# A complex scan over 63 chunk states rebuilt as a tree, with its transposes and spills moved, in a one-core decoder layer

## What is computed

```python
def combine(e1, e2):
    a1r, a1i, b1r, b1i = e1
    a2r, a2i, b2r, b2i = e2
    return (a2r * a1r - a2i * a1i, a2r * a1i + a2i * a1r,
            a2r * b1r - a2i * b1i + b2r, a2r * b1i + a2i * b1r + b2i)
_, _, hr, hi = lax.associative_scan(combine, (ar_full, ai_full, bu_re, bu_im), axis=1)
y = einsum('btgp,gcp->btgc', hr, c_re) - einsum('btgp,gcp->btgc', hi, c_im)
...
y_act = gelu(y_ssm)
```

## Time and profile before

| what | value |
|---|---|
| median of three runs | 922.96 us (922.57 to 925.85) |
| the profiled execution | 927.62 us, its span 925.9 us |
| PE busy (matmul) | 906.0 us, 98% of the span |
| PE busy (weight loads) | 882.5 us, 95% |
| DVE busy | 603.8 us, 65% |
| ACT busy | 443.2 us, 48% |
| POOL busy | 97.0 us, 10% |
| mean granted clock of TensorE | 0.996 |

### The profile page before, as it was taken

The page is one execution under the profiler, slowest core; times in us unless marked ns, Lnnn a source line. Parts: engine busy times, 40 slices in busy tenths (PEclk is TensorE's granted clock), DMA queues, the critical chain, the costliest instruction groups (busy, mean ns, idle before and its releaser), DMA issues.

```text
span 925.9 us, 17543 instructions
## 1 busy us (share of the span) xinstructions
PE 906.0 (98%) x7350; PEld 882.5 (95%) x7350; DVE 603.8 (65%) x815; ACT 443.2 (48%) x663; POOL 97.0 (10%) x151
## 2 busy tenths in 40 slices
PE   6999999998999999999999999999999999999998
PEld 5999998998999889999999999999999999999998
DVE  6689699810777746474568666666676666778453
ACT  7446333233876544544356544444444444446532
POOL 5390036102001210100000000000000000000000
PEclk9999999999999999999999999999999999999999
DMA  8521579844423576522323322223323223242202
GB/s 229 131 83 45 155 214 189 198 117 131 124 72 100 194 274 217 171 69 71 90 69 92 92 88 83 86 88 91 92 76 94 84 91 91 92 137 71 70 4 99
DMA packets 135333, 105.71 MB, mean 114 GB/s; under 512 B 18688, under 2 KB 124536, under 8 KB 134968
## 3 DMA queue, kind: packets, MB, share of 16 engines
q1 hardware_dynamic: 129096, 83.38, 30.6%
q0 software_dynamic: 6064, 21.19, 8.0%
q10 hardware_dynamic: 96, 0.04, 0.0%
HBM read 90.48 MB, written 13.98 MB: 113 GB/s over the span
## 4 chain that ended last, share of the span: by engine, by line
PE 88%; DVE 6%; ACT 3%; issue 1%; DMA 1%; SPq 0%; ACTq 0%; DVEq 0%; POOLq 0%
PE dense L2324 62%; PE banks L2324 19%; PE scoreA L2324 3%; PE banks L2511 2%; DVE Hb L1750 1%; DVE sc L1750 1%; DMA xtok<-in_x_prompt 1%; PE scoreB L2324 1%; ACT whi L1361 1%; DVE wlo L1774 1%; DVE Llo L1774 1%; ACT t L1655 1%; DVE t L2148 1%; DMA y_spill<-ygelu 0%; DVE Ssum L1750 0%
## 5 line engine op out<-in xcount | busy, mean ns | idle before, releaser
L1774 DVE TENSOR_TENSOR wlo<-wraw,whi 128x1024 fp32r<-128x1024 f32 (+2 forms) x139 | 152.7, 1103 | 108.9 <-ACT whi L1361 96.9
L2324 PE MATMUL dense<-hid,whi 128*128 128x256 f32 (+1 forms) x1024 | 176.5, 294 | 0.1
L2324 PE MATMUL dense<-act_hi,whi 128*128 128x256 f32 (+1 forms) x736 | 168.5, 300 | 2.5 <-DVE wlo L1774 2.2
L2324 PE MATMUL dense<-act_hi,wlo 128*128 128x256 f32 (+1 forms) x736 | 164.5, 295 | 0.0
L2324 PE MATMUL dense<-act_lo,whi 128*128 128x256 f32 (+1 forms) x736 | 164.3, 295 | 0.0
L2324 PEld LDWEIGHTS dense<-hid,whi 128*128 128x128 f32 x1024 | 152.3, 187 | 0.5 <-issue 0.5
L1361 ACT CAST whi<-wraw 128x1024 fp32r<-128x1024 f32 x100 | 109.9, 1101 | 45.6 <-PE banks L2324 44.1
L2324 PEld LDWEIGHTS dense<-act_hi,whi 128*128 128x128 f32 x736 | 125.0, 190 | 5.7 <-DVE wlo L1774 2.4
L2324 PEld LDWEIGHTS dense<-act_lo,whi 128*128 128x128 f32 x736 | 125.3, 189 | 0.0
L2324 PEld LDWEIGHTS dense<-act_hi,wlo 128*128 128x128 f32 x736 | 125.1, 189 | 0.0
L2324 PE MATMUL dense<-hid,wlo 128*128 128x256 f32 (+1 forms) x512 | 108.8, 293 | 0.0
(11 more groups left out here) (375 smaller groups left out, 1592.9 us busy)
## 6 DMA issues: line engine op xcount, KB each, us to landing
wraw<-in_w_in SPq DMA_DIRECT2D x32, 512.0 KB, 5.7
wraw<-in_w_up SPq DMA_DIRECT2D x32, 512.0 KB, 4.1
wraw<-in_w_down SPq DMA_DIRECT2D x32, 512.0 KB, 4.2
gates_spill<-gst POOLq DMA_DIRECT2D x16, 288.0 KB, 3.3
page<-in_cache_k SPq DMA_DIRECT2D x16, 256.0 KB, 8.7
page<-in_cache_v SPq DMA_DIRECT2D x16, 256.0 KB, 7.3
wraw<-in_w_out SPq DMA_DIRECT2D x8, 512.0 KB, 4.1
wraw<-in_w_ple_gate SPq DMA_DIRECT2D x8, 512.0 KB, 4.1
```

Of the source, the lines that this page charges most:

```text
L1774: return nc.vector.tensor_tensor(out=lo, in0=whole, in1=f32(hi), op=ALU.subtract)
L2324: return nc.tensor.matmul(out, lhsT, rhs, start=start, stop=stop, skip_group_check=True)
```

## The change

The scan becomes a tree: five levels up (distance 1 to 16) and five down (16 to 1), each over every 2d-th position only. Up, the destinations are 2d, 4d, ...; down, 3d, 5d, .... The counts n are 31, 15, 7, 3, 1 and 1, 3, 7, 15, 31, together 114. The ten steps are spread over the same five first places of the schedule as (0), (1, 2), (3, 4, 5, 6), (7, 8), (9), and the sixth place has none; `final` moves up by one place. The states go out after unit 18, and come in after unit 20; two whole units that stood between them and the first `y` now stand behind `sfinal`, ahead of the `vout` transposes. After the last `y` the first half of a unit is begun. POOL makes one power less, and the counts awaited on `scanned` follow.

```diff
+SCANS = 10
...
-        event("scan", lvl)
-        if lvl == 5:
+        for step in ((0,), (1, 2), (3, 4, 5, 6), (7, 8), (9,), ())[lvl]:
+            event("scan", step)
+        if lvl == 4:
             event("final")
         unit()
...
+        if lvl == 4:
+            event("swap_out", "states")
         if lvl in (3, 4):
             unit()
-    event("swap_out", "states")
     event("swap_in", "states")
-    unit()
-    unit()
     begin(4)
     for q in range(4):
         for side in range(2):
             event("y", q, side, place=2 * (q % 2) + side)
         if q % 2 == 0:
             unit()
-        elif q == 1:
+        else:
             begin(4)
+        if q == 1:
             event("pairqk", 0)
     event("sfinal", place=0)
+    unit()
+    unit()
+    only.append(DENSE)
     for t in range(5):
         event("vout", t, place=t % 4)
-    only.append(DENSE)
     unit()
...
-                    for n in range(5):
+                    for n in range(SCANS // 2 - 1):
...
-                            pool.wait_ge(scanned, 7)
+                            pool.wait_ge(scanned, SCANS + 1)
...
-                    lvl = a[0]
+                    up = a[0] < SCANS // 2
+                    lvl = a[0] if up else SCANS - 1 - a[0]
                     d = 1 << lvl
-                    n = NPC - 1 - d
-                    if lvl == 0:
+                    first = 2 * d if up else 3 * d
+                    n = len(range(first, NPC, 2 * d))
+                    if a[0] == 0:
                         vector.wait_ge(*reached["squares"])
...
-                    src = Hb[:, :, :, 1:1 + n]
+                    src = Hb[:, :, :, first - d:NPC - d:2 * d]
...
-                    dst = Hb[:, :, :, 1 + d:NPC]
+                    dst = Hb[:, :, :, first:NPC:2 * d]
...
-                    vector.wait_ge(scanned, 7)
+                    vector.wait_ge(scanned, SCANS + 1)
```

## The result

The changed kernel takes 927.99 us (median of 17 runs, 926.75 to 931.57), the kernel before, on the same chips, 923.65 us (17 runs, 922.02 to 927.0). The ratio is 1.0046, with a 95% interval of 1.0035 to 1.0058: slower by 0.46%, inside the 0.5% that counts here as no change, but outside the predicted 913.3 to 921.8 us and on the other side of the kernel before.

A forecast was written before the change was run, and what follows sets the result against it. PE, busy in 98% of the span, was taken as the bound. Waits and clock worth 9.3 us, less 3.9 us for a new wait, give 5.4 us won; scaled to the median, 917.6 us, range 913.3 to 921.8 us.

The forecast's parts named there:

- the wait at the scan: PE's 2.19 us wait for the low part of unit 19 goes, with 1.6 us of clock: 3.8 us won.
- Both waits at v: PE's waits of 0.82 and 3.04 us before the transposes of v go, with 1.6 us of clock: 5.5 us.
- The stores are seen landed: States stored behind the loads of Tm and gate spills in POOL's queue: moving from about 168.2, seen landed at 172.1.
- the wait that takes its place: At the first y PE waits 2.3 us for late states; with 1.6 us of clock this costs 3.9 us.
- The load of the states, 4.9 + 0.8 us: Loading the states takes 4.9 us, plus 0.8 us for sharing with half a weight load: in at 177.8.
- the second rival: Wait at the first y is 5.0 us, two weight loads being ahead: 2.7 us won, 920.3 us; chance 0.2.
- The clock behind that wait, 1.6 us: Low clock behind the new wait at the first y, charged as behind the old 2.19 us wait: 1.6 us.
- What there is to win, 9.3 us: Waits and clock removed at the scan (3.8 us) and at v (5.5 us): 9.3 us, 1.0% of the kernel.
- The first (states in time): States arrive in time for the first y, so all 9.3 us are won: 913.7 us; chance 0.2.
- The third: Small strided rows on DVE cost four cycles an element instead of two: slower, 934 us; chance 0.05.
- The fourth: Waits go, but work behind them stays put and attention starts as before: 923 us; chance 0.05.
- The point from which the change loses: The change loses once the states land 7.7 us after PE asks for them at the first y.

The follow-up runs named there:

- the version without the exchange: Changed kernel without the four DMAs that store and reload the states through DRAM; y waits for the scan and uses unexchanged states: 917.13 us, ratio 0.9931.
- before, again: The kernel before, unchanged, run and profiled a second time: 923.25 us, ratio 0.9997.
- the tree alone: Changed kernel with y and the transposes of v back in their old places; tree scan and early exchange of states stay: 922.58 us, ratio 0.9985.
- one unit back: Changed kernel with one of the two moved units put back ahead of the first y: 918.89 us, ratio 0.9945.
- loads ahead of gate spill: Changed kernel with the loads of the states ahead of the gate spill of unit 19 in POOL's queue: 928.01 us, ratio 1.0038.
- weights held from 27: Changed kernel with SP's weight loads of units 27 and later held until the states have landed: 925.69 us, ratio 1.0007.
- states on ScalarE's queue: Changed kernel with the four DMAs of the states issued by ScalarE on its own queue, right behind unit 18: 922.92 us, ratio 0.9991.
- wait ahead of the blocks: Changed kernel with PE's wait for the states moved ahead of the four input blocks of a unit before the first y: 928.72 us, ratio 1.0043.
- weights held from 24: Changed kernel with weight loads from unit 24 on held until Tm is in, and from 27 on until the states are in: 924.19 us, ratio 1.0007.
- moves with the old scan: Against the kernel before: old six-level scan kept, only y, the two units and the transposes of v moved as in the change: 935.9 us, ratio 1.0128.
- tree, v one unit later: Changed kernel with y in its old place and the transposes of v one unit later than in the kernel before: 917.6 us, ratio 0.993.
- one unit back, weights held: Changed kernel with one moved unit back ahead of y and weight loads from unit 24 on held until Tm is in: 917.35 us, ratio 0.9928.

## Why the prediction was wrong

**The ledger.** The profiled executions can be added up, to about 1 us, from the version without the exchange (916.99 us) plus PE's waits in the stretch and half of the busy time behind them at the low clock:

| kernel | waits | clock | sum | its profiled execution |
|---|---|---|---|---|
| before | 2.2 + 0.8 + 3.0 | 1.6 + 1.6 | 926.2 | 927.62 |
| before, again | 2.2 + 0.8 + 2.2 | 1.6 | 923.8 | 924.54 |
| changed | 5.5 | 4.5 | 927.0 | 926.75 |
| the tree alone | 1.0 + 0.8 | 0 | 918.8 | 919.61 |
| one unit back | 0.9 | 0 | 917.9 | 919.14 |
| loads ahead of gate spill | 1.0 + 6.3 | 5.6 | 929.9 | 930.28 |
| weights held from 27 | 1.5 + 3.0 | 3.4 | 924.9 | 925.54 |
| states on ScalarE's queue | 4.0 | 1.7 | 922.7 | 922.89 |
| wait ahead of the blocks | 8.9 | 2.4 | 928.3 | 928.35 |
| weights held from 24 | 3.1 | 3.4 | 923.5 | 923.3 |
| moves with the old scan | 2.2 + 9.3 | 1.5 + 5.3 | 935.3 | 935.49 |
| tree, v one unit later | 0 | 0 | 917.0 | 917.77 |
| one unit back, weights held | 0 | 0 | 917.0 | 917.52 |

The clock terms are from windows at 0.50 to 0.56: for the weights held, 6.83 us at 0.50, which begin 1.4 and 1.9 us after PE has resumed; for the moves with the old scan, 10.53 us at 0.50 behind `y` and 3.05 at the scan; for the loads ahead of the gate spill, 11.39 us at 0.51. The sums lie within 1.4 us of the executions, six of thirteen within 0.5 us, and eleven are below them, by 0.1 to 1.4 us. So the waits and the clock of this stretch carry all but about 1 us of every version; what the rest is was not looked for.

**What held.** The tree costs DVE what was said: steps of 31, 15 and 7 positions take 4.9, 4.3 and 2.4 us (predicted 4.85, 4.7, 2.6), those of 3 and 1 take 1.4 and 0.9 (1.6 and 1.1), but for the 2.8 us of step 5. The low part of unit 19 comes at 155.7 (156.3 to 158.1), ahead of PE, and the wait at the scan is gone with its clock. `scanned` is full at about 162.6 (163.2 to 165.0 predicted). PE asks for the states at 174.4 (175.5). Both waits at v are gone; no kernel with v behind later units has one. That the states would be late for `y`, and that this sets the result, held too.

**What was luck.** The stores are seen landed at 171.8, and 172.1 was predicted, but not by this way. The prediction took the issue of `Tm` from the trace of before ("`Tm` can't come sooner"); it came 2.7 us sooner, at 152.56. And it held the stores back by their place behind the backlog in POOL's queue; on a queue of their own they are as late, and with the weight loads held they are seen landed at 169.0. An error of 2.7 us and a cost of 3 us for weight loads that the term did not have cancel each other.

**What failed: the size of the wait that takes its place.** Three terms of the sum:

1. *The load of the states, 4.9 + 0.8 us.* It takes 8.1 us. The step that failed is the conclusion that weight loads stand back behind POOL's transfers. In the kernel before, weight loads got nothing for 5 us and took 9.3 us to land, and I charged half of one load. The kernel after shows both: q1 has no packet from 156 to 161, beside `Tm`, but it takes 86% of the engines' time from 161 to 166, and moves 1.08 MB beside 0.88 MB of q0 from 172 to 180. With the loads from unit 27 on held the leg is 4.8 us, as before the change; with other weight loads held into it, 8.7 us. The wait became 5.5 us, not 2.3: this is the wait of the second rival (5.0 us), and its sharing is what the holds show. The Trainium skill (DMA: Bandwidth & Descriptors, "Queues, rings and completion order") has each engine going round-robin between queues, packet by packet; by that rule the prediction had worked out that second rival. The traces agree with it in the windows 161 to 166 and 172 to 180, where both queues move, and not from 156 to 161. The same page ("Rules for kernel authors") says that spreading DMAs over the issuing engines does not raise bandwidth; the 9.1 us of the stores on ScalarE's queue agree. Why q1 moves nothing beside `Tm`, in the kernel before (162 to 167) and after (156 to 161), stays open.

2. *The clock behind that wait, 1.6 us.* It is 4.3 to 4.5 us. I took the price of the 2.19 us wait, behind which PE ran 3.46 us at the low clock. Behind this one it ran 8.95 us, of a low stretch of 10.24. With the same late states and the wait ahead of the four blocks the low stretch is as long, but 5.4 us of it lie inside the wait of 8.9 us and 2.4 us are lost; with `y` behind the wait 3.4 us are lost even after 3.0 us. So the price of the 2.19 us wait did not carry over, not even to a wait near the predicted 2.3; whether the length of the wait or the work behind it makes the stretch long was not separated. The second rival had this term at 1.6 as well, and so gave 920.3 us.

3. *What there is to win, 9.3 us.* It came from one execution, and its 5.5 us at v include a fall of the clock that other executions don't have; another execution of the same kernel had 3.0 there, and without the exchange the median falls by 6.4 us. I scaled the total to the median, by 0.995, which leaves the gain at 9.3 us, but 2.4 of the 4.7 us by which that execution stood above the median were part of that gain.

Together: predicted 9.3 - 3.9 = 5.4 us won; by the medians 6.4 - 10.6 = 4.2 us lost, which is the measured 0.46%. The wait at `y` with its clock is 10.0 us in the profiled execution, the fastest one; the median execution is 1.2 us slower, at a lower mean clock. The larger error is in the second half, 6 to 7 us; the first is 3 us.

**The rivals.** The first (states in time) is what the version without the exchange shows, except that it wins 6.4 us and not 9.3. The third fell with the strided rows: the steps of 15 and 7 positions took 4.3 and 2.4 us, less than the 4.7 and 2.6 that two cycles an element had given. The fourth did not happen: with no wait at `y` the kernel ends 6 us sooner. The point from which the change loses, states 7.7 us after PE asks, was worked out with 1.6 us of clock and 9.3 us of gain; with 6.4 us of gain and the clock's real price it lies near 3 us of waiting (3.1 us of wait and 3.4 of clock come out even, ratio 1.0007).

**What stays open.** Where the six longer runs of the tree alone lose their 3 to 7 us, beyond the lower mean clock that they have, and what decides in a given execution whether the clock falls. What makes the low stretch longer behind some waits. Why q1 has no packet beside `Tm`. And why the gate spill's landing (10.8 us median from 157 on) is longer than in the kernel before (8.0): sharing with the weight loads explains the direction, but it was not measured by itself.

## What to carry to other kernels

When a producer moves earlier and its consumer moves earlier by as much, a round trip through DRAM between them no longer has the empty stretch that it had: price it by what else the DMA engines carry at the new time, and if it is late, leave one unit of work ahead of the consumer or hold the other queue's loads until the data it needs first has landed; holding them shifts their cost to whatever is next. A wait on PE has a second price, the work that runs at the low clock behind it, and that price can't be taken from another wait: here it was 1.6 us behind 2.2 us of waiting, 3.4 behind 3.0, 4.5 behind 5.5 and 2.4 behind 8.9. And the gain of a removed wait is sized from several executions: a fall of the clock behind it may be in one of them and not in the next.

## What the runs showed of the hardware

- The low clock of a fall covered 4.8 us of work behind a wait of 8.9 us, 9.0 us behind a wait of 5.5, and 10.5 us behind one of 9.3. In the first two the low stretch as a whole was equally long, 10.1 and 10.2 us, and they differ by what of it passed inside the wait.
- A kernel's executions differ in their falls of the clock: of 73 of the kernel before, 25 have a mean granted clock of 0.999 or 1.000, 39 of 0.997 or 0.998, and 9 of 0.996 or less.
- In float32 tensor operations on DVE, a step of 8 bytes was free: the step of 31 positions takes 4.9 us so, and 4.85 us packed, in level 5 of the old scan. A step of 16 bytes was not: 480 elements took 0.97 us in the products of step 1. The formula of the packed levels gives 2.8 us for that step, which took 4.3. The Trainium skill (SBUF — State Buffer, "Door 1: The DMA port swizzle") asks for at least two hits in a 16-byte line for full bandwidth. In float32 a step of 8 bytes gives two and a step of 16 bytes one, so these rows agree.
- A queue of its own gave a transfer no speed: the stores took 9.0 us from POOL and 9.1 us from ScalarE, and 6.0 us once the weight loads were held.
- Weight loads beside POOL's transfers got no packet for 5 us in one stretch (156 to 161 of the kernel after, beside the loads of `Tm`), and 86% of the engines' time in the next (161 to 166).
- POOL's two operations on 16 by 512 elements took 1.05 and 1.29 us beside DVE operations of 32 elements a partition, and 2.76 and 3.07 us beside those of the old scan's level 2, of 1888 and 944.
